# Memory keys and values of a hybrid encoder: values by token, ahead of the keys

## The reference, cut to what matters

```
def cross_attention(h, m, w_q, w_kv, w_o, q_norm, k_norm):
    q = rms_norm((h @ w_q).reshape(bsz, L, X_HEADS, X_DH), q_norm) * (X_DH ** -0.5)
    kv = (m @ w_kv).reshape(bsz, m.shape[1], 2, X_HEADS, X_DH)
    k = rms_norm(kv[:, :, 0], k_norm)
    v = kv[:, :, 1]
    p = softmax(einsum('bqhd,bmhd->bhqm', q, k))
    o = einsum('bhqm,bmhd->bqhd', p, v).reshape(bsz, L, D_MODEL)
    return o @ w_o

    # in each layer:
    m = rms_norm(mem, p['norm_mem'][layer])
    x = x + cross_attention(h, m, ...)
```

## Time and profile before

| | before |
|---|---|
| median of 3 runs | 2372.33 us (2371.93 to 2372.36) |
| span of the profiled execution | 2370.0 us; the runs' median is 2.33 above it |
| PE, PE weight load, DVE, ACT busy | 100%, 85%, 66%, 50% |
| granted TensorE clock | 1.000 (of the 2.4 GHz level) |
| 200 to 300 us: PE, DVE, ACT busy | 99.07, 76.64, 48.24 us |
| 300 to 400 us | 97.42, 77.11, 51.96 us |
| 400 to 450 us | 50.00, 38.43, 24.06 us |
| 450 to 500 us | 49.99, 42.49, 39.66 us |

### The profile page before, as it was taken

The page is one execution under the profiler, slowest core; times in us unless marked ns, Lnnn a source line. Parts: engine busy times, 40 slices in busy tenths (PEclk is TensorE's granted clock), DMA queues, the critical chain, the costliest instruction groups (busy, mean ns, idle before and its releaser), DMA issues.

```text
span 2370.0 us, 34640 instructions
## 1 busy us (share of the span) xinstructions
PE 2358.6 (100%) x13711; PEld 2005.1 (85%) x13711; DVE 1572.6 (66%) x2666; ACT 1187.2 (50%) x2106; POOL 0.2 (0%) x4
## 2 busy tenths in 40 slices
PE   9999999999999999999999999999999999999999
PEld 6888877888889888987788888888888898888888
DVE  8999668776687776664665548858985575433332
ACT  6334455555445565545463536646874453433432
POOL 0000000000000000000000000000000000000000
PEclk9999999999999999999999999999999999999999
DMA  5346633553224664443225223233334324333332
GB/s 203 100 103 179 210 110 107 165 204 117 71 89 152 194 187 133 134 137 105 78 98 169 89 92 122 90 106 99 98 100 151 116 88 126 115 98 98 98 98 89
DMA packets 110273, 291.63 MB, mean 123 GB/s; under 512 B 18976, under 2 KB 41248, under 8 KB 108832
## 3 DMA queue, kind: packets, MB, share of 16 engines
q1 hardware_dynamic: 101552, 265.68, 35.6%
q10 hardware_dynamic: 8560, 23.73, 3.2%
HBM read 267.48 MB, written 19.79 MB: 121 GB/s over the span
## 4 chain that ended last, share of the span: by engine, by line
PE 87%; DVE 2%; ACT 1%; issue 0%; DMA 0%; SPq 0%; ACTq 0%
PE ps L1613 64%; PE ps L1590 5%; PE ps L1636 3%; PE ps L1595 3%; PE ps L1758 2%; PE ps L1707 2%; PE ps L1785 2%; PE ps L1738 1%; PE ps L1773 1%; PE ps L1722 0%; PE ps L2208 0%; PE ps L2275 0%; PE ps L1652 0%; DVE wlo L1563 0%; PE ps L1669 0%
## 5 line engine op out<-in xcount | busy, mean ns | idle before, releaser
L1558 ACT ACTIVATE whi<-wraw 128x1024 fp32r<-128x1024 f32 x430 | 451.9, 1052 | 202.6 <-PE ps L1613 125.5
L1563 DVE TENSOR_TENSOR wlo<-wraw,whi 128x1024 fp32r<-128x1024 f32 x430 | 522.1, 1217 | 8.0 <-ACT whi L1558 7.8
L1613 PE MATMUL ps<-in_hP,whi 128*128 128x512 f32 x1272 | 505.7, 398 | 1.7 <-DVE in_lP L2092 0.8
L1613 PE MATMUL ps<-in_hP,wlo 128*128 128x512 f32 x1272 | 495.8, 390 | 0.0
L1613 PE MATMUL ps<-in_lP,whi 128*128 128x512 f32 x1272 | 495.4, 389 | 0.0
L1613 PE MATMUL ps<-hid_P,whi 128*128 128x512 f32 x1008 | 311.8, 390 | 0.0
L1613 PEld LDWEIGHTS ps<-in_hP,whi 128*128 128x128 f32 x1272 | 238.8, 188 | 56.6 <-issue 4.8
L1613 PEld LDWEIGHTS ps<-in_hP,wlo 128*128 128x128 f32 x1272 | 238.7, 188 | 50.6
L1613 PEld LDWEIGHTS ps<-in_lP,whi 128*128 128x128 f32 x1272 | 239.0, 188 | 49.3 <-issue 1.4
L2014 DVE TENSOR_TENSOR x<-ps,x 128x256 f32<-128x256 f32 (+1 forms) x191 | 106.1, 555 | 253.9 <-PE ps L1613 252.3
L1613 PE MATMUL ps<-in_S,whi 128*128 128x256 f32 x1408 | 260.9, 287 | 0.0
(11 more groups left out here) (544 smaller groups left out, 3764.7 us busy)
## 6 DMA issues: line engine op xcount, KB each, us to landing
wraw<-wt SPq DMA_DIRECT2D x432, 512.0 KB, 3.5
wraw<-wt ACTq DMA_DIRECT2D x16, 512.0 KB, 4.2
k_scratch<-region_P SPq DMA_DIRECT2D x16, 256.0 KB, 3.2
v_scratch<-vtmp SPq DMA_DIRECT2D x32, 128.0 KB, 3.4
x<-x_in SPq DMA_DIRECT2D x4, 768.0 KB, 6.9
x<-x_in SPq DMA_DIRECT2D x2, 1536.0 KB, 7.3
mix_mem<-mem_in ACTq DMA_DIRECT2D x1, 2048.0 KB, 15.6
region_S<-k_scratch ACTq DMA_DIRECT2D x2, 1024.0 KB, 6.7
```

Source lines behind the costliest of these rows:

```text
L1558: nc.scalar.activation(whi[:, (n + 3) % NHI, :, :], wraw[:, ws(n), :, :], ACT.Copy).then_inc(wh.sem, 1)
L1563: nc.vector.tensor_tensor(wlo[:, ws(n), :, :], wraw[:, ws(n), :, :], whi[:, (n + 3) % NHI, :, :].bitcast(F32), ALU.subtract).then_inc(wr.s ...
L1613: last = nc.tensor.matmul(ps[:, bank(m), 0:N[prod.g]], w_[:, k, :], x_[:, k, :], start=(k == 0 and j == 0), stop=(k == KT - 1 and j == 2))
```

## The change

Values are made with the tokens on the partitions at once. A value weight tile no longer holds 128 columns for all 1024 features but 512 columns for 256 features (`by_token`, on the host). A block of 128 memory tokens (in_hP, in_lP) is the stationary operand and 512 weight columns are moving; four tiles in a row add up in four banks (`MEM_BANKS` 7, 2, 0, 1, one for each block of tokens), and two such halves f = 0, 1 make a layer's values. A tile is still 24 matmuls of 128 x 512. At the fourth tile ACT empties two of the banks and DVE two, into `vtmp` and the second half of `ktmp`, and SP stores four pieces of 256 KB. Ring copies, transposes and their copies are gone. In both layers the eight value tiles now come first, then the eight key tiles. Since bank 7 is taken, the GLA's values of an even unit go to bank 6 and wait for `wrd` (its weighted scores) before both halves; the finish of S head 3 starts one slot later; the lambda product of layer 1 moves to bank 5. (after.py's L1631 is L1613 of before, L1709 and L1710 are L1660 and L1661, L1713 is L1664, L2028 to L2030 are L1977 to L1979, L2114 is L2054, L2527 to L2529 are L2462 to L2464, L1576 is L1563, L2092 is L2032, L2130 is L2075, L2140 is L2085, L2065 is L2014, L2263 is L2208.) The core of the diff:

```diff
-KV_ORDER = [i for h in range(4) for i in (2 * h, 2 * h + 1, 8 + 2 * h, 9 + 2 * h)]
-KV_ORDERS = [KV_ORDER, KV_ORDER[:8] + [4, 5, 6, 7] + list(range(12, 16))]
+KV_ORDER = list(range(8, 16)) + list(range(8))
...
+                def evicted(self, f, b):
+                    n = 2 * f + b // 2 + 1
+                    return (gs["P"]["vca"].sem, self.vca + n) if b % 2 == 0 else (gs["P"]["vcp"].sem, self.vcp + n)
...
+            def is_value(prod, i):
+                return prod.kind == "mem" and i >= KT
+            def mem_stage(b):
+                return vtmp[:, b, :] if b < 2 else ktmp[:, 1, b - 2, :]
...
-                attach(27 if h == 3 else 13 + 2 * h, [[("fin", gl["S"], h, 0)], [("fin", gl["S"], h, 1)]])
+                attach(28 if h == 3 else 13 + 2 * h, [[("fin", gl["S"], h, 0)], [("fin", gl["S"], h, 1)]])
...
-                    z, h = gs["P"], i % KT // 2
-                    if i < KT:
-                        sp.wait_ge(z["ksc"].sem, mk.ksc + h + 1)
-                    else:
-                        sp.wait_ge(z["vcp"].sem, mk.vcp + i - KT + 1)
+                    z, h, f = gs["P"], i // 2, i // 4 - 2
+                    if i >= KT:
+                        for b in range(4):
+                            sp.wait_ge(*mk.evicted(f, b))
+                            sp.dma_start(v_dram[mk.layer, b // 2].rearrange("p (j d) -> p j d", j=2)[:, b % 2, 512 * f:512 * f + 512],
+                                         mem_stage(b)).then_inc(vout[b // 2].sem, 16)
+                        return
+                    sp.wait_ge(z["ksc"].sem, mk.ksc + h + 1)
...
+                if is_value(prod, i):
+                    pe_mem_values(pe, t, middle)
+                    return
+                if prod.kind == "mem" and i < 2:
+                    pe.wait_ge(*prod.evicted(1, MEM_BANKS.index(bank(m))))
...
+            def pe_mem_values(pe, t, middle):
+                prod, i, m = t
+                z, f, kk = gs["P"], i // 4 - 2, i % 4
+                flat_h, flat_l = (w_.rearrange("p k n -> p (k n)") for w_ in (whi[:, (m + 3) % NHI], wlo[:, ws(m)]))
+                h_, l_ = prod.rhs
+                for b in range(4):
+                    if b == 2 and middle is not None:
+                        pe_states(pe, middle)
+                    if f == 0 and kk == 0:
+                        if b == 0:
+                            pe.wait_ge(gs["F"]["snew"].sem, gl["S"].stats[2].new)
+                        elif b == 1:
+                            pe_bank(pe, prod.evicted(1, 1))
+                        else:
+                            pe.wait_ge(tf[MEM_BANKS[b]].sem, (banked[m] + 1 - MEM_BANKS[b]) // 2)
+                    if f == 1 and kk == 0:
+                        pe.wait_ge(*prod.evicted(0, b))
+                        if b == 1 and prod.layer == 0:
+                            pe_bank(pe, prod.evicted(1, 1))
+                    to = slice(b * P, b * P + P)
+                    for e in range(2):
+                        k, cs = 2 * kk + e, slice(512 * e, 512 * e + 512)
+                        if f == 0 and b == 0 and prod.ready is not None:
+                            pe.wait_ge(*prod.ready(k))
+                        for j, (x_, w_) in enumerate(((h_, flat_h), (h_, flat_l), (l_, flat_h))):
+                            last = nc.tensor.matmul(ps[:, MEM_BANKS[b], :], x_[:, k, to], w_[:, cs],
+                                                    start=(k == 0 and j == 0), stop=(k == KT - 1 and j == 2))
+                    if kk == 3 and b < 3:
+                        last.then_inc(z["vtr"].sem, 1)
+                last.then_inc(td.sem, 1)
...
-                if prod.kind == "mem" and i >= KT:
-                    pe_bank(pe, (z["vcp"].sem, prod.vcp + i - KT + 1))
-                    pe.wait_ge(tf[bank(m)].sem, use(m) + 1)
-                    for b in range(4):
-                        last = nc.tensor.transpose(ps[:, 2, b * P:(b + 1) * P], ring[g][:, i % 2, b * P:(b + 1) * P], ident)
-                    last.then_inc(z["vtr"].sem, 1)
...
+                elif is_value(prod, i):
+                    if i % 4 == 3:
+                        f = i // 4 - 2
+                        for b_ in (0, 2):
+                            a.wait_ge(z["vtr"].sem, prod.vtr + 3 * f + b_ + 1)
+                            mem_stage_free(a, prod, f, b_)
+                            nc.scalar.activation(mem_stage(b_), ps[:, MEM_BANKS[b_], :], ACT.Copy).then_inc(z["vca"].sem, 1)
...
+                elif is_value(prod, i) and i % 4 == 3:
+                    f = i // 4 - 2
+                    for b_ in (1, 3):
+                        if b_ < 3:
+                            v.wait_ge(z["vtr"].sem, prod.vtr + 3 * f + b_ + 1)
+                        else:
+                            v.wait_ge(td.sem, m + 1)
+                        mem_stage_free(v, prod, f, b_)
+                        nc.vector.tensor_copy(mem_stage(b_), ps[:, MEM_BANKS[b_], :]).then_inc(z["vcp"].sem, 1)
...
-                if prod.kind == "mem" and i >= KT:
-                    v.wait_ge(z["vtr"].sem, prod.vtr + i - KT + 1)
-                    if prod.layer or i >= KT + 2:
-                        v.wait_ge(vout[i % 2].sem, prod.layer * 16 * KT + 32 * ((i - KT) // 2))
-                    nc.vector.tensor_copy(vtmp[:, i % 2, :], ps[:, 2, :]).then_inc(z["vcp"].sem, 1)
...
-            def o_ps(hh):
-                return ps[:, 5 if hh else 7, :]
+            def o_ps(u, hh):
+                if hh:
+                    return ps[:, 5, :]
+                return ps[:, 7 if u.i % 2 else 6, :]
             def pe_values(pe, u):
+                if u.i == 1:
+                    pe.wait_ge(*m0.evicted(1, 0))
+                elif u.i == 3:
+                    pe.wait_ge(gs["F"]["snew"].sem, gl["S"].stats[3].new)
                 for hh in range(2):
-                    if hh == 1:
+                    if hh == 1 or u.i % 2 == 0:
...
+    for n in ("din", "kv0", "kv1"):
+        parts[n] = _np.concatenate([parts[n][:-KT], by_token(late[n][:, -D:])], 0)
```

More of the change, by code:

```diff
@@ L766, in _ @@
                     pe.wait_ge(tf.sem, 2 * NT)
[L767 to L771, removed]
+                    pe.wait_ge(vcopied.sem, 4)
+                    flat_h, flat_l = (w_.rearrange("p k n -> p (k n)") for w_ in (whi[:, 3], wlo[:, NT % NRAW]))
+                    for b in range(4):
+                        to = slice(b * P, b * P + P)
+                        for k in range(2):
+                            if b == 0:
+                                pe.wait_ge(mar.sem, k + 1)
+                            cs = slice(512 * k, 512 * k + 512)
+                            for j, (x_, w_) in enumerate(((in_hP, flat_h), (in_hP, flat_l), (in_lP, flat_h))):
+                                last = nc.tensor.matmul(ps[:, MEM_BANKS[b], :], x_[:, k, to], w_[:, cs],
+                                                        start=(k == 0 and j == 0), stop=False)
                     last.then_inc(td_tail.sem, 1)
@@ L1484, in trunk_tail @@
             for prod, i, m in tiles:
-                banked.append(banked[-1] + (prod.kind != "vtok"))
+                banked.append(banked[-1] + (prod.kind != "vtok" and not is_value(prod, i)))
             def bank(m):
@@ L1496, in trunk_tail @@
                     outs[m] = (prod.g, i)
-                if prod.kind == "mem" and (i % 2 == 1 or i >= KT):
+                if prod.kind == "mem" and i % (4 if i >= KT else 2) == (3 if i >= KT else 1):
                     kvs[m] = (prod, i)
@@ L1842, in act_tile @@
-                    if i < KT:
-                        nc.scalar.activation(ring[g][:, j, :], acc_ps, ACT.Square).then_inc(z["sqd"].sem, 1)
-                        if prod.layer or h >= 2:
-                            a.wait_ge(kout[h % 2].sem, prod.layer * 16 * XH + 32 * (h // 2))
-                        nc.scalar.activation(ktmp[:, h % 2, j, :], acc_ps, ACT.Copy).then_inc(tf[b].sem, 1)
-                    else:
-                        nc.scalar.activation(ring[g][:, j, :], acc_ps, ACT.Copy).then_inc(tf[b].sem, 1)
+                    if h >= 1:
+                        if j == 0 and prod.layer:
+                            a.wait_ge(z["kad"].sem, prod.kad + h)
+                        else:
+                            a.wait_ge(z["ssum"].sem, prod.stats[h - 1].sum)
@@ L1849, in act_tile @@
+                    nc.scalar.activation(ring[g][:, j, :], acc_ps, ACT.Square).then_inc(z["sqd"].sem, 1)
+                    if prod.layer or h >= 2:
+                        a.wait_ge(kout[h % 2].sem, prod.layer * 16 * XH + 32 * (h // 2))
+                    if i == 2:
+                        a.wait_ge(vout[1].sem, 64 * prod.layer + 64)
+                    nc.scalar.activation(ktmp[:, h % 2, j, :], acc_ps, ACT.Copy).then_inc(tf[b].sem, 1)
                 elif prod.kind == "q":
```

59 lines of the change are left out of this document (30 added, 29 removed).

## The result

The changed kernel takes 2378.95 us (median of 6 runs, 2378.38 to 2379.95) against 2372.06 of the kernel before (6 runs): ratio 1.0029, interval 1.0019 to 1.0039. It is slower by 6.9 us. The forecast was 2376.2, just inside what can't be told from no change; the time lies in the range for 8 in 10 (2368.5 to 2381), but outside the forecast's own (2374.5 to 2377.7). Two executions, one of 6068.78 us of the kernel before and one of 3519.57 us in run 6, are far slower than all others of the same kernel and left out of the ratios.

A forecast was written before the change was run, and what follows sets the result against it. TensorE was taken as busy throughout, with ACT's and DVE's chains setting the time at places A, B and C; 2370.0 + 3.9 = 2373.9 us of span, plus 2.33, gave 2376.2 us; own range 2374.5 to 2377.7, 8 in 10: 2368.5 to 2381.

The forecast's parts named there:

- What goes: Memory stage: 64 transposes leave, 7.04 us of TensorE, with ring copies and a 1.3 us wait; 8.3 us if nothing else moved.
- What stays: Value tiles remain 24 matmuls with operands swapped, priced at 0; copies and bank emptying 0, or 1 us if DVE is late.
- Place A: End of layer 0's memory, now a key tile: TensorE stands still 3.3 us, where it stood 1.3; GLU begins about 329.8.
- Place B: Chain to GLA unit 2: first normalisation at 336.1, TensorE idles some 4 us more, transposes end 1.3 us later.
- T: End of layer 1's 13th tile: 455.05 us before, forecast at 454.6.
- place C: Finish of the GLA heads P behind T: DVE's work ends with the second addition to x at 490.0; TensorE starts 3.9 later.
- The sum: Whole kernel: 2370.0 + 3.9 = 2373.9 us of span, 2376.2 us of time, 0.16% slower.
- The 3.9: At place C, TensorE's next tile starts 3.9 us later than before (486.14), and nothing behind gives it back.
- rival of 0.08: Clock falls to the 1.2 GHz level behind an idle at A, B or C: +5.5 us, 2381.7, slower; chance 0.08.
- SP's queue: Last key pair's store holds up weight loads behind it in SP's order: up to 3.5 us more, 2379.7; chance 0.12.
- Place C does not bind: DVE keeps pace at the finish of the GLA heads P: 2371.9 us, no change; chance 0.31.
- The transposes show: DVE and ACT overlap more at A, B and C, so 7.04 + 1.3 us come off, 2364.0; chance 0.09.

The follow-up runs named there:

- run 6: Changed kernel with the moves of run 3 and run 4 together, the scaling of layer 0's last key pair at the start of slot 21: 2371.94 us.
- run 1: Kernel before, with one of the four transposes of each value tile kept, so its values are wrong: 2366.6 us, ratio 0.9976.
- run 4: Changed kernel, layer 0's last key pair: ones product and root behind the first GLU product and activation, stat before second S finish, scaling behind layer 1's second tile: 2376.52 us.
- run 5: Changed kernel with unread matmuls filling three TensorE waits (ones product, unit 2's transposes, eo tile; the last group 11, ahead of the weights wait): 2375.57 us.
- run 3: Changed kernel, with stat and scaling of layer 1's last key pair, and its store, moved behind the first eo tile of P: 2373.28 us, ratio 1.0005.
- runs 9 and 10: Run 6 with layer 0's last pair's root directly behind its ones product, scaling behind unit 2's step; 10 adds 6 unread matmuls: 2375.29 and 2375.65 us.

## Why the prediction was right or wrong

- **What goes.** The 7.04 us of transposes were priced right: three quarters of them, 5.3 us, are worth 5.7 in the old order (run 1). Wrong was the reading beside it, that TensorE "only happens to be late enough to hide" a chain of its own: the chain is released by TensorE and moves with it, so that the gain was not hidden in the kernel before.
- **What stays.** The value tiles, whose copies and operands were priced at 0, show no wait over 0.8 us, and their products took 389 ns (median in the changed kernel's trace), as the earlier trace rows had it.
- **Place A.** Forecast: TensorE stands still for 3.3 us, the GLU begins at 329.8. Measured: 3.7, and 330.3. With the ones product moved (run 4) the wait is gone. That the order does this, and not the new form of the values, follows from the list on TensorE; no run had the new order with the old values.
- **Place B.** Forecast: L2140 at 336.1 (335.6 by the rows alone), the transposes' end at 375.6. Measured: 335.55 and 375.7. That the end agrees so well is in part luck: the start was 0.55 earlier than taken, and the slow GLU gave about as much back; in run 5, with the clock at 1.00, L2140 began at 336.00 and the transposes ended at 375.22. The wait there was 2.5 us and not 4, because the GLU had slowed TensorE by 2.4 us in the meantime. The wait for the weighted scores is 0.88 (0.9).
- **T and place C.** Forecast: T at 454.6, the second addition to x ending at 490.0, the next tile at about 490. Measured: 456.3, 491.7 and 491.86, each 1.7 to 1.9 late. This comes ahead of T, nearly all of it (1.6) from the slow tile at place B; the step itself (T to the end of the addition) was forecast as 35.4 and took 35.4. Run 3 shows that the stat and scaling of the last pair are what decides.
- **The sum.** It gave 2373.9 us of span for DVE's delays. With the waits filled, and so with the delays alone, the span is 2373.8 (run 5), with T at 454.2 and the next tile at 489.75. (The 3.9 sets the addition's end, 490.0, against the tile's start before, 486.14; like for like it is 0.1 to 0.2 more, which changes nothing.) What failed is the step that left the clock out of the sum: it stood as a rival of 0.08, tied to +5.5 us. It cost 3.4 us by the medians of run 5 (2378.95 to 2375.57), 3.2 by the profiles: 0.5 by way of the GLU at place A, 1.6 in the tile at place B, 1.1 behind place C. It came behind all three waits, not instead of the forecast but on top of it. So the prediction's own last sign of being wrong, a granted clock under 1.00 behind one of the idles, is there, although the time lies in the range.
- **The ground for the low chance.** It was that no row showed the clock fall, the longest wait being 2.5 us. That wait was no guide. It runs from the start of the span to TensorE's first matmul, so that nothing had been running:

```profile
2.51 10.56 PE L388 MATMUL ps<-mix_h 128*128 128x512 f32 x33 [2.51 <-DVE mix_h L856]
```

And the waits at place B, 2.2 and 0.35 us, are together no longer than that, and the clock behind them was 0.76 all the same (374 to 378 us). The Trainium skill (TensorE: Matmul & The Clock Gate, section Loop structure matters more than you think) says that a long wait between matmuls leaves TensorE cold; its example is a wait for DMA in each round of a loop. This trace agrees, for single waits that DVE ends: granted clock 0.97, 0.87 and 0.94 from 300 to 380 us, 0.91 from 480 to 500.
- **The rivals.** SP's queue did not bind in the changed kernel (no wait in TensorE's list is ended by a transfer); it did in runs 9 and 10, by a store that my own edit had put late. "Place C does not bind" is refuted by the 3.3 us of wait at 491.86. "The transposes show" is refuted for this order and true for the old one.

What stays open: why the same wait of 3.7 us at place A cost different amounts in two profiles (the GLU's first 32 matmuls took 12.94 us in the changed kernel, 11.39 in run 3), so that what a single wait costs by the clock is known here to about 1 us only; and how the values by token would do in the old order, which no run tried.

## What to carry to other kernels

In the old order a saving on the busiest engine was worth its full size (run 1); in the new one the side chains spent it. Check, for each piece that is moved to the end of a stage, who must wait for its last step and what used to stand between. When an edit makes TensorE wait for some microseconds in mid-stream (2.2 to 3.7 here), price the matmuls behind the wait at the lower clock as well, in the sum and not as a rival. A step that is put late takes its store with it, and whoever reuses the store's buffer waits for both.

## What the runs showed that I had not expected

The same DVE delays cost 2375.57 us with TensorE kept busy in its waits and 2378.95 without, on one core alone. Unread matmuls behind a wait, not in it, gained nothing and ran slowly themselves (13 in 4.63 us; 14 in 3.57 in a wait). And one tile of 24 matmuls took 6.94 us behind a wait of 3.1 us, and 5.50 with that wait filled up to 1.4.
